# Two of four weight sums by accumulating transfers instead of VectorE, in the seven-product blocks of a feed-forward

## The reference

```python
D_FF_2 = 4 * D_MODEL                      # 8192, D_MODEL = 2048, SEQ = 256
...
    h = rms_norm(x, norm_mlp_pre[l])
    u = jnp.square(jax.nn.relu(h @ w_up[l]))
    x = x + rms_norm(u @ w_down[l], norm_mlp_post[l])
```

## Time and profile before

| | us |
|---|---|
| median of 3 runs | 2473.54 (2473.47 to 2473.64) |
| span of the profiled execution, first to last instruction | 2471.7 |
| median less span | 1.8 |
| PE busy | 2462.0 |
| DVE busy | 1635.3 |
| ACT busy | 1246.5 |
| POOL busy | 46.6 |

### The profile page before, as it was taken

One profiled execution on the slowest core, in us unless ns is written; L12 is line 12 of the kernel. 1 busy time (PEld: TensorE's weight loads), 2 busy tenths in 40 slices (PEclk: granted clock), 3 DMA queues, 4 the chain that ended last, 5 costly groups with the idle time before them and its releaser, 6 DMA issues.

```text
span 2471.7 us, 32412 instructions
## 1 busy us (share of the span) xinstructions
PE 2462.0 (100%) x12464; PEld 2088.6 (85%) x12464; DVE 1635.3 (66%) x1954; ACT 1246.5 (50%) x1606; POOL 46.6 (2%) x74
## 2 busy tenths in 40 slices
PE   9999999999999999999999999999999999999998
PEld 8888888888888888888888788888888888888887
DVE  5756767655767467755775457755667668678676
ACT  6444556545565355544555445444644445444453
POOL 0100100000000000000000000000000000000000
PEclk9999999999999999999999999999999999999999
DMA  9655565655655555565557565555565655656563
GB/s 326 209 187 172 169 171 174 226 184 173 191 192 197 189 186 187 188 203 188 186 200 250 157 205 166 162 171 174 167 207 188 198 193 190 199 174 221 187 210 131
DMA packets 251987, 472.57 MB, mean 191 GB/s; under 512 B 23344, under 2 KB 26928, under 8 KB 251232
## 3 DMA queue, kind: packets, MB, share of 16 engines
q1 hardware_dynamic: 251728, 470.98, 58.1%
q10 hardware_dynamic: 144, 0.03, 0.0%
HBM read 468.85 MB, written 2.13 MB: 191 GB/s over the span
## 4 chain that ended last, share of the span: by engine, by line
PE 99%; DVE 1%; ACT 0%; issue 0%; DVEq 0%; POOLq 0%; ACTq 0%
PE psum L2189 21%; PE psum L2098 19%; PE psum L2100 19%; PE psum L2099 19%; PE psum L2197 11%; PE psum L2154 1%; PE psum L2715 1%; PE psum L2716 1%; PE psum L2717 1%; PE psum L2159 1%; PE psum L2214 1%; PE psum L2260 0%; PE psum L2282 0%; PE psum L2308 0%; PE psum L2116 0%; PE psum L2115 0%
## 5 line engine op out<-in xcount | busy, mean ns | idle before, releaser
L1343 DVE TENSOR_TENSOR wl<-raw,wh 128x1024 fp32r<-128x1024 f32 x596 | 729.7, 1227 | 576.7 <-ACT wh L844 575.3
L844 ACT ACTIVATE wh<-raw 128x1024 fp32r<-128x1024 f32 x596 | 624.1, 1057 | 575.2 <-PE psum L2100 389.0
L2098 PE MATMUL psum<-wh,ha 128*128 128x512 f32 x1584 | 630.7, 398 | 0.0
L2100 PE MATMUL psum<-wh,ha 128*128 128x512 f32 x1584 | 618.4, 390 | 0.0
L2099 PE MATMUL psum<-wl,ha 128*128 128x512 f32 x1584 | 617.9, 390 | 0.0
L836 ACT ACTIVATE wh<-raw 128x1024 fp32r<-128x1024 f32 x249 | 261.0, 1060 | 319.6 <-PE psum L2100 137.4
L1339 DVE TENSOR_TENSOR wl<-raw,wh 128x1024 fp32r<-128x1024 f32 x249 | 302.5, 1224 | 173.2 <-ACT wh L836 169.3
L2100 PEld LDWEIGHTS psum<-wh,ha 128*128 128x128 f32 x1584 | 297.6, 188 | 63.6
L2098 PEld LDWEIGHTS psum<-wh,ha 128*128 128x128 f32 x1584 | 298.0, 188 | 60.5 <-issue 2.6
L2099 PEld LDWEIGHTS psum<-wl,ha 128*128 128x128 f32 x1584 | 298.2, 188 | 57.6
L2189 PE MATMUL psum<-ha,wh 128*128 128x512 f32 x1344 | 313.1, 390 | 0.0
(11 more groups left out here) (310 smaller groups left out, 1960.4 us busy)
## 6 DMA issues: line engine op xcount, KB each, us to landing
raw<-in_w_up SPq DMA_DIRECT2D x152, 1024.0 KB, 5.1
raw<-in_w_in SPq DMA_DIRECT2D x116, 1024.0 KB, 5.1
raw<-in_w_down SPq DMA_DIRECT2D x108, 1024.0 KB, 5.0
raw<-in_w_out SPq DMA_DIRECT2D x32, 1024.0 KB, 4.9
raw<-in_w_branch_a SPq DMA_DIRECT2D x8, 1024.0 KB, 4.9
raw<-in_w_branch_b SPq DMA_DIRECT2D x8, 1024.0 KB, 5.0
raw<-in_w_in SPq DMA_DIRECT2D x5, 512.0 KB, 8.2
x_t<-in_x_t SPq DMA_DIRECT2D x8, 256.0 KB, 6.4
```

What stands on the lines that cost most here:

```text
L844: act.activation(wh[q % SPLIT_SLOTS][:], raw[q // 2 % RAW_SLOTS][:, 2 * (q % 2):2 * (q % 2) + 2, :], ACT.Copy).then_inc(hi_done, 1)
L1343: dve.tensor_tensor(wl[q % SPLIT_SLOTS][:], raw[q // 2 % RAW_SLOTS][:, 2 * (q % 2):2 * (q % 2) + 2, :], wh[q % SPLIT_SLOTS][:].bitcast(F32 ...
L2098: pe.matmul(acc, hi, wh[s][:, c, :], start=first and c == 0, stop=False)
L2100: ins = pe.matmul(acc, lo, wh[s][:, c, :], start=False, stop=last and c == 1)
```

## The change

The third and fourth weight sums leave VectorE. GpSimd's queue first copies `b22` and `b21` into `w_sum[2]` and `w_sum[3]`, once both slots have landed. When VectorE has made `w_sum[0]`, GpSimd issues a transfer that adds `w_sum[0]` to `w_sum[2]`, waits until it has landed, and issues one that adds `w_sum[2]` to `w_sum[3]`. Since the scheme's differences of weights become plain additions, signs move: to two of the sums of activations, and to the additions in `shared_products`. ScalarE's rounding of the third and fourth sums waits for those transfers (`third_in`, `fourth_in`). The two slots are free one step earlier than before, and SP's next loads into them also wait for the copies (`copy_in`). To have three semaphores, small loads at the start (`ident`, part of `params`) count on `heads_in`, and one ScalarE wait uses its chain's semaphore.

```diff
-SUM_STEPS = ((3, 4, 5, 5), (2, 3, 4, 5))
+SUM_STEPS = ((3, 4), (2, 3))
...
     if r in (3, 4):
-        return first + max(SUM_STEPS[pair]) + 1 + AHEAD + 1
+        return first + max(SUM_STEPS[pair][-1] + AHEAD + 2, SEVEN + 3)
...
             sp.wait_ge(lo_done, load_done(u - RAW_SLOTS))
+            old = u - RAW_SLOTS - LOADS_BEFORE
+            if old >= 0:
+                op, r = divmod(old, 32)
+                pair, r = divmod(r - 16, 8)
+                if pair >= 0 and r in (3, 4) and not is_plain(op, pair):
+                    sp.wait_ge(sem["copy_in"], 32 * (2 * op + pair + 1))
...
+        def chained_sums(k):
+
+            p, pair = divmod(k, 2)
+            u = LOADS_BEFORE + 32 * p + 16 + 8 * pair + 3
+            for v in (u, u + 1):
+                pool.wait_ge(raw_in[v % RAW_SLOTS], 16 * (v // RAW_SLOTS + 1))
+            if k:
+                last = S_DOWN2[(k - 1) // 2] + N_PAIR * ((k - 1) % 2) + SEVEN + 6
+                pool.wait_ge(lo_done, last + 1)
+            pool.dma_start(w_sum[2][:], raw[(u + 1) % RAW_SLOTS][:, 2:4, :]).then_inc(sem["copy_in"], 16)
+            pool.dma_start(w_sum[3][:], raw[u % RAW_SLOTS][:, 2:4, :]).then_inc(sem["copy_in"], 16)
+            pool.wait_ge(sem["copy_in"], 32 * (k + 1))
+            pool.wait_ge(sem["sum_ok"], 2 * k + 1)
+            pool.dma_start(w_sum[2][:], w_sum[0][:], accum_op=ALU.add).then_inc(sem["third_in"], 16)
+            pool.wait_ge(sem["third_in"], 16 * (k + 1))
+            pool.dma_start(w_sum[3][:], w_sum[2][:], accum_op=ALU.add).then_inc(sem["fourth_in"], 16)
+
+        for k in range(2 * UP2_PASSES - 1):
+            chained_sums(k)
...
                 if u is None:
-                    act.wait_ge(sem["sum_ok"], sums_before(q) + part + 1)
+                    k = sevens_before(q)
+                    if part < 2:
+                        act.wait_ge(sem["sum_ok"], 2 * k + part + 1)
+                    else:
+                        act.wait_ge(sem["third_in" if part == 2 else "fourth_in"], 16 * (k + 1))
...
-                chain.link(dve.tensor_tensor(a_sum[:, 0], a21, a22, ALU.add))
-                chain.link(dve.tensor_tensor(a_sum[:, 1], a_sum[:, 0], a11, ALU.subtract))
+                chain.link(dve.tensor_tensor(a_sum[:, 0], a22, a21, ALU.subtract))
+                chain.link(dve.scalar_tensor_tensor(a_sum[:, 1], a_sum[:, 0], -1.0, a11, ALU.mult, ALU.subtract))
...
-            made = 8 * p + 4 * pair
-            if n == 2:
-                dve.wait_ge(sem["sum_ok"], made + 1)
-            if n == 3:
-                dve.wait_ge(sem["sum_ok"], made + 3)
-            plus, minus = ((b12, b11), (b22, b12), (b22, w_sum[0][:]), (b21, w_sum[2][:]))[n]
-            dve.tensor_tensor(w_sum[n][:], plus, minus, ALU.subtract).then_inc(sem["sum_ok"], 1)
+            if n == 0 and (p, pair) != (0, 0):
+                dve.wait_ge(sem["third_in"], 16 * (2 * p + pair))
+            dve.tensor_tensor(w_sum[n][:], b12, (b11, b22)[n], ALU.add).then_inc(sem["sum_ok"], 1)
...
                 if p:
                     dve.tensor_tensor(y21, u3, y21, ALU.add)
-                    dve.tensor_tensor(y12, u4, y12, ALU.add)
-                chain.link(dve.tensor_tensor(u2 if p else y22, e[1], u3, ALU.add))
+                    dve.tensor_tensor(y12, y12, u4, ALU.subtract)
+                    chain.link(dve.tensor_tensor(u2, e[1], u3, ALU.add))
+                else:
+                    chain.link(dve.scalar_tensor_tensor(y22, e[1], -1.0, u3, ALU.mult, ALU.subtract))
...
-                    for k in range(4):
+                    for k in range(2):
                         if n == SUM_STEPS[pair][k]:
                             weight_sum(p, pair, k)
```

More of the change, by code:

```diff
@@ L411, in build @@
     names = """
-      par_in par_rest warm_set xt_hi xt_lo ident_in hi_first lo_first rot_in heads_in near_in xre_in
+      par_in warm_set xt_hi xt_lo hi_first lo_first rot_in heads_in near_in xre_in
       hi_done lo_done mm_done row_free chan_free
-      act_chain dve_chain pool_chain consts_set act_warm
+      act_chain dve_chain pool_chain consts_set
       norm_ss norm_rs tr_full tr_hi tr_lo scales_out rstd_row_ok gained
@@ L425, in build @@
       rtab_in rope_ok silu_g rq_mm rq_ok rk_mm rk_ok rs_mm rp_ok ro_mm ro_stat ro_rs ro_ok ro_gated
-      first_tile post_first tile0_full tile0_hi tile0_lo post_ok last_gained y_last sum_ok first_copied extra_free var_ok grow_in out_in cmask_in
+      first_tile post_first tile0_full tile0_hi tile0_lo post_ok last_gained y_last sum_ok first_copied extra_free copy_in third_in fourth_in var_ok grow_in out_in cmask_in
     """.split()
@@ L488, in sums_made, with sevens_before @@
         return (c + 3) // 4
-    def sums_before(q):
+    def sevens_before(q):
         p, r = divmod(q - S_UP2[0], PASS_STEPS)
-        return 8 * p + 4 * ((r - 32) // N_PAIR)
+        return 2 * p + (r - 32) // N_PAIR
     def causal(n):
@@ L578, in _ @@
             elif j == 0:
-                sp.dma_start(ident[:], a["ident"]).then_inc(sem["ident_in"], 16)
-                sp.dma_start(par[:, Q_BQ:Q_COLS], a["params"][:, Q_BQ:Q_COLS]).then_inc(sem["par_rest"], 16)
+                sp.dma_start(ident[:], a["ident"]).then_inc(sem["heads_in"], 16)
+                sp.dma_start(par[:, Q_BQ:Q_COLS], a["params"][:, Q_BQ:Q_COLS]).then_inc(sem["heads_in"], 16)
             elif j == 1:
@@ L987, in _ @@
         act.wait_ge(sem["consts_set"], 1)
-        act.activation(squares[:, 0:32], neghalf[:], ACT.Copy).then_inc(sem["act_warm"], 1)
-        act.wait_ge(sem["act_warm"], 1)
+        chain.link(act.activation(squares[:, 0:32], neghalf[:], ACT.Copy))
         for q in range(FINE_SPLITS):
@@ L1016, in split_outputs @@
                            ).then_inc(sem["ot_hi"], 1)
-        act.wait_ge(sem["heads_in"], 32)
-        act.wait_ge(sem["par_rest"], 16)
+        act.wait_ge(sem["heads_in"], 64)
         for s in range(8 * GATE_BLOCKS):
@@ L1554, in split_outputs @@
                               ha[:, 2 * c:2 * c + 2, 0, :].bitcast(F32), ALU.subtract).then_inc(sem["ot_lo"], 1)
-        dve.wait_ge(sem["heads_in"], 32)
-        dve.wait_ge(sem["par_rest"], 16)
+        dve.wait_ge(sem["heads_in"], 64)
         for s in range(8 * GATE_BLOCKS):
@@ L1947, in up2_stage @@
                 dve.wait_ge(sem["act_ready"], 11 + c + 1 + sums_made(c))
-                chain.link(dve.tensor_tensor(a_sum[:, 0], a21, a22, ALU.add))
-                chain.link(dve.tensor_tensor(a_sum[:, 1], a_sum[:, 0], a11, ALU.subtract))
+                chain.link(dve.tensor_tensor(a_sum[:, 0], a22, a21, ALU.subtract))
+                chain.link(dve.scalar_tensor_tensor(a_sum[:, 1], a_sum[:, 0], -1.0, a11, ALU.mult, ALU.subtract))
                 dve.tensor_tensor(a_sum[:, 2], a11, a21, ALU.subtract)
-                dve.tensor_tensor(a_sum[:, 3], a12, a_sum[:, 1], ALU.subtract).then_inc(sem["act_ready"], 1)
+                dve.tensor_tensor(a_sum[:, 3], a12, a_sum[:, 1], ALU.add).then_inc(sem["act_ready"], 1)
             if j == 7 and c % 4 == 0:
@@ L1991, in shared_products @@
             if n == 1:
-                dve.tensor_tensor(u4, e[1], u2, ALU.add)
+                if p:
+                    dve.tensor_tensor(u4, e[1], u2, ALU.add)
+                else:
+                    dve.scalar_tensor_tensor(y12, e[1], -1.0, u2, ALU.mult, ALU.subtract)
                 chain.link(dve.tensor_tensor(u3, e[3], u2, ALU.add))
@@ L1996, in shared_products @@
                     dve.tensor_tensor(y21, u3, y21, ALU.add)
-                    dve.tensor_tensor(y12, u4, y12, ALU.add)
-                chain.link(dve.tensor_tensor(u2 if p else y22, e[1], u3, ALU.add))
+                    dve.tensor_tensor(y12, y12, u4, ALU.subtract)
+                    chain.link(dve.tensor_tensor(u2, e[1], u3, ALU.add))
+                else:
+                    chain.link(dve.scalar_tensor_tensor(y22, e[1], -1.0, u3, ALU.mult, ALU.subtract))
                 dve.sem_inc(sem["extra_free"], 1)
             if n == 3 and p:
-                chain.link(dve.tensor_tensor(y22, u2, y22, ALU.add))
+                chain.link(dve.tensor_tensor(y22, y22, u2, ALU.subtract))
         def add_block(p, b, steps):
@@ L2321, in _ @@
         row_blocks(S_IN1 + 8, R_IN1 + 1, IN1_BLOCKS - 1, 8, ha)
-        pe.wait_ge(sem["ident_in"], 16)
+        pe.wait_ge(sem["heads_in"], 64)
         for s in range(8 * GATE_BLOCKS):
```

## The result

The changed kernel takes 2526.88 us (median of 4 runs, 2525.91 to 2528.47) against 2473.51 us before on the same chip (4 runs): ratio 1.0216, 95% interval 1.0204 to 1.0229. It is 53.4 us slower. The direction was forecast; the size is four times the forecast, and the time lies above the range. The profiled execution took 2525.91 us with a span of 2524.1 us, 52.4 us more than before.

The account below looks back on a forecast made before the run. TensorE was taken as the bound, busy 2462.0 of 2471.7 us. Transfer stalls of 4 x 2.6 + 3 x 1.2 = 14.0 us, less 1.1 gained, gave +12.9 on 2473.54: 2486.4 us, range 2472 to 2512.

Parts of the forecast that it names:

- The bound of the gain: TensorE's waits for VectorE in the seven products: 0.27 us in each of 4 even pairs, at most 1.1 us to win.
- The windows: Time from the first sum's end until the fourth must be in memory: 10.1 us in even pairs, 12.8 in odd.
- The place: Sign: ScalarE's rounding waits for a DMA on the sums, PE's weight loads for low parts in step 12, not 9.
- An accumulate alone: One 512 KB accumulating transfer on idle DMA engines: 5.0 us like a 1 MB load plus 0.71 issue, 5.7 us.
- VectorE's operations: Sign: if DVE's operations of 1.22 us grow while GpSimd issues, something other than the chain is at work.
- The sign for late copies: If the first accumulate starts later than 0.2 us after the first sum, the copies caused it.
- the loads beside the second accumulate: Two 1 MB loads in an even pair lengthen the second accumulate by 1.3 us, to 7.0 us.
- the forecast stall of 2.6: Even pair: accumulates of 5.7 + 7.0 = 12.7 us overrun the 10.1 us window, stalling 2.6 us in each of four.
- the copies: Two copies filling the accumulators take 4.1 to 7.7 us, covered in even pairs, up to 0.6 late in odd ones.
- the forecast 1.2: Odd pair: accumulates of 7.0 + 7.0 = 14.0 us overrun the 12.8 us window, stalling 1.2 us in each of three.
- Much lateness: Rival: an accumulate's reads and writes do not overlap, 9.4 us each, stalls of 52.8 us, 2525 us in all; chance 0.17.
- The fitting chain: Rival: both transfers land within 10.1 us of the first sum, no stall, 2472.4 us; chance 0.39 including nearly fitting.

Follow-up runs that it names:

- the version without any wait: The change with loads held until both accumulates landed, accumulators filled from HBM, first sum one step earlier in even pairs: 2472.54 us against 2473.64, ratio 0.9996.
- the run without transfers: Kernel before, all four sums on VectorE, the fourth held back by 9 or 10 GpSimd clearings of a spare tile: 2528.55 us, ratio 1.0222.
- the run with waits of 2.3 us: Kernel before, all four sums on VectorE, the fourth held back by 6 or 7 GpSimd clearings of a spare tile: 2496.52 us, ratio 1.0091.

## Why the prediction was wrong in size

**What held.** The bound of the gain, 1.1 us: the version without any wait is 1.1 us under the kernel before, in the medians. The windows, 10.1 and 12.8 us: subtracted from the measured chains they give PE's waits to within 0.4 us in each of the seven pairs. (The matmul at 1880.04 that the earlier trace rows calls step 11's is in the second half of step 10; only its 0.22 us behind its weight load was used, so the window stands.) The place: ScalarE's rounding waits for the transfer, PE in step 12 and not in step 9. An accumulate alone: priced 5.7 with its issue, measured 4.5, issue included, so 1.2 too dear; that it occupies the engines like 1 MB, 2.6 us, came out. VectorE's operations did not grow. The sign for late copies, a start of the first accumulate more than 0.2 us behind the first sum, was set too low: it starts 0.56 us behind the sum in the first even pair, where no copy is late.

**The step that failed first: the loads beside the second accumulate.** The prediction saw that the earlier release puts two 1 MB loads beside it and added 1.3 us, half of what the accumulate's 1 MB takes at 406 GB/s, with 2.6 as the upper end. Measured: 10.0 in the first even pair against 4.5 with the loads held back, 5.5 more. The prediction also read in the earlier trace rows that the first accumulate of an even pair is alone; the copies push the load before it into its way, which cost up to 1.2 us (landings of 4.5 to 5.7 in even pairs, 4.5 alone). The upper end was drawn from the accumulate's own bytes, as if the engines shared evenly by bytes and the accumulate paid at most for itself; two loads cost it about their whole 5.2 us. In the first even pair this term alone turns the forecast stall of 2.6 into 5.1; in the three others (5.4 to 5.7) a later start or a longer first accumulate adds 0.7 to 1.2. In odd pairs, too, the forecast 1.2 became 4.2 to 5.5: of that, the second accumulate is 9.4 - 7.0 = 2.4 in the first of them, the start behind the sum 3.1 (0.56 of it without any late copy), and the first accumulate 6.15 against 7.0 gives 0.9 back. In sum 36.6 us of waits against 14.0, so 22.6 us of what the forecast lacked.

**The second step: the copies.** They were priced at 4.1 to 7.7 us for two and called covered. The view of the waits puts the first accumulate down to them in six of seven pairs. Its start says five: 3.1, 1.5, 1.3, 2.7 and 1.1 us behind the first sum, but 0.56 and 0.55 in the first and second even pairs. In the first odd pair the copies take from 1910.87 to 1920.26, 9.4 us for two. The price was low, but with the loads in place it decides little: 4.8 us.

**The step that was missing: the clock.** The prediction took a wait of PE for its own length. Every one of its waits here, 4.2 us and more, was followed by some us at 1.2 GHz, and PE's busy time grew by 15.5 us, 2.2 a pair, all of it missing from the forecast; the run without transfers shows the same, 17.9 us behind 37.2 us of waits. With this term the forecast's own stalls of 2.6 us would have cost up to an estimated 2.1 us more in each even pair, by the run with waits of 2.3 us. The Trainium skill, "TensorE: Matmul & The Clock Gate", section "What's actually happening", says that a gate passes only a share of TensorE's clock pulses, depending on how busy PE has been recently, and so names what these rows show; the slices at 0.50 and the matmuls 0.43 us apart agree.

**The rivals.** Much lateness, 2525 us, had the time, but not for its reason. That rival was an accumulate whose reads and writes do not overlap, 9.4 us each wherever it runs; measured were 4.5 alone, and a plain copy beside the loads takes 9.0 in the first even pair as well. Its sum had 52.8 us of PE waits, the kernel has 36.6 and the rest is the clock. The fitting chain came true where the loads are held back: 2476.6 to 2472.5 us. The fit quoted from the Trainium skill, "DMA: Bandwidth & Descriptors", section "Anatomy of one DMA — SWDGE (gpsimd) path", gave an estimate of 3.2 us for a plain 512 KB; the trace agrees, 3.2 us where a plain copy found the engines nearly at rest. With the two source reads of an add, from "Collectives: The Full Stack" of the Trainium skill, the estimate was 4.4; the trace agrees here too, 4.4 to 4.5 alone. So the accumulate alone was priced well by these estimates and too dear by the prediction; the 5.5 us for the loads beside it, which the prediction put at 1.3, are in neither estimate.

**What stays open.** How the DMA engines choose between GpSimd's transfer and SP's loads, so that two loads cost 5.5 us and one 1.4; and why the clock fell after three of seven waits of nearly the same length (in the run with plain copies after one of 3.18 us, too, but not after one of 3.13).

## What to carry to other kernels

A stall of TensorE can have two prices, its length and the matmuls behind it at the lower clock (here with every stall of 4.2 us and more of the change, and with none of the stalls, 1.5 us at most, of the run with the loads held back); count both, and test the second with a wait that is made without the suspected cause. When a change moves work to a transfer that sits on the path, list every load that an edit releases at that moment: here a release one step earlier, meant as no more than bookkeeping of slots, was 36 of 53 us. A transfer that is called alone is worth a look at the DMA share while it runs: the first pair's 4.7 and 5.0 us hid that the add costs 1.3. Before moving work off an engine, read how long the bottleneck waits for that engine; here it was 1.1 us, and no version could win more.

## What the runs showed of the hardware that was not expected

A transfer of 512 KB within SBUF from GpSimd's queue that accumulates lands 4.4 to 4.5 us after its issue when alone, and fills the DMA engines at 201 GB/s; a plain one that found them nearly at rest landed after 3.2 us and moved at 391 GB/s. Issuing takes GpSimd 0.53 us plain and 0.86 to 0.95 accumulating. Beside two 1 MB loads of SP's queue the accumulate takes 9.3 to 10.1 us, beside one 5.9 in the first even pair. TensorE's granted clock fell to 0.50 after each idle time of 4.2 us and more in the change, and after three of seven of 2.2 to 2.3 us.
